# Output projections between the layers of a two-block network: seven half-size fp32 products instead of eight, the token tiles in two pairs

## The reference

```python
for layer in range(4):          # mixers: latent attention, window attention, Hyena, latent attention
    hx = rmsnorm(x, g_pre[layer]) * (1.0 + scale_x) + shift_x       # same for ctx
    yx, yc = mixer(hx, hc, ..., w_out)     # ends in (o * silu(gate)) @ w_out, w_out is 1024 x 1024
    x = x + gate_x * rmsnorm(yx, g_post[layer])
    ctx = ctx + gate_c * rmsnorm(yc, g_post[layer])                 # not in the last layer
```

## Time and profile before

| what | value |
|---|---|
| median of 3 runs | 1885.49 us (1885.35 to 1885.64) |
| span of the profiled execution | 1879.6 us, so 5.9 us below the median of the runs |
| TensorE busy | 1825.9 us, 97% |
| VectorE busy | 824.3 us, 44% |
| ScalarE busy | 412.2 us, 22% |
| GpSimd busy | 65.8 us, 4% |
| matmuls of L714 | 166.6 us |
| DMA queue | 366.36 MB |

### The profile page before, as it was taken

How to read it: one execution, slowest core, us unless ns; L and a number is a source line. 1 busy time by engine, 2 the same in 40 slices (tenths; PEclk the granted TensorE clock), 3 DMA queues, 4 the chain that set the end, 5 groups by cost and what they waited for, 6 DMA issues and landing times.

```text
span 1879.6 us, 18030 instructions
## 1 busy us (share of the span) xinstructions
PE 1825.9 (97%) x6829; PEld 960.0 (51%) x6829; DVE 824.3 (44%) x2070; ACT 412.2 (22%) x1011; POOL 65.8 (4%) x82
## 2 busy tenths in 40 slices
PE   6999999999999999999899999999999999999997
PEld 2545564444454744443345855588854443443432
DVE  4874545773775666527953233363441010010001
ACT  2121342102772222112212223222111111111111
POOL 0000000000100000004500000000010000000000
PEclk9999999999999999999999999999999999999999
DMA  9754100552100534321203330534487999999993
GB/s 403 263 208 181 45 1 23 213 204 109 68 1 14 208 113 157 123 101 45 73 1 146 133 124 1 201 124 151 157 352 293 427 428 427 428 427 428 428 427 166
DMA packets 31398, 367.57 MB, mean 196 GB/s; under 512 B 3675, under 2 KB 3788, under 8 KB 6348
## 3 DMA queue, kind: packets, MB, share of 16 engines
q1 hardware_dynamic: 31308, 366.36, 48.7%
HBM read 365.26 MB, written 1.09 MB: 195 GB/s over the span
## 4 chain that ended last, share of the span: by engine, by line
PE 93%; DVE 4%; ACT 1%; issue 1%; DMA 1%; POOL 0%; SPq 0%; DVEq 0%; ACTq 0%; POOLq 0%
PE bank L812 14%; PE bank L2967 12%; PE bank L714 9%; PE bank L1790 8%; PE bank L3004 6%; PE bank L1620 4%; PE bank L1337 3%; PE bank L2988 3%; PE bank L895 3%; PE bank L2942 3%; PE bank L2265 2%; PE bank L1465 2%; PE bank L917 2%; PE bank L1175 1%; PE bank L2771 1%; PE bank L1503 1%
## 5 line engine op out<-in xcount | busy, mean ns | idle before, releaser
L812 PE MATMUL bank<-hT,slot 128*128 128x256 f32 (+1 forms) x832 | 268.1, 478 | 0.4 <-DVE open_o L835 0.4
L812 PEld LDWEIGHTS bank<-hT,slot 128*128 128x128 f32 x832 | 156.0, 190 | 97.7 <-issue 85.0
L407 DVE SCALAR_TENSOR_TENSOR product<-slot,cond_rows 128x1024 f32<-128x1024 f32 x160 | 195.6, 1223 | 8.6 <-DVE product L407 3.0
L1790 PE MATMUL bank<-hT,slot 128*128 128x512 f32 (+1 forms) x448 | 168.9, 531 | 0.0
L714 PE MATMUL bank<-slot,gT 128*128 128x512 f32 x384 | 166.6, 592 | 0.0
L3044 DVE SCALAR_TENSOR_TENSOR hT<-hT,bank 128x512 f32<-128x512 f32 x16 | 11.0, 688 | 259.8 <-ACT hT L3079 259.8
L1790 PEld LDWEIGHTS bank<-hT,slot 128*128 128x128 f32 x448 | 83.2, 190 | 70.1 <-issue 67.0
L714 PEld LDWEIGHTS bank<-slot,gT 128*128 128x128 f32 x384 | 72.3, 190 | 88.0 <-issue 87.9
L3004 PE MATMUL bank<-slot,hT 128*64 128x512 f32 x256 | 92.1, 595 | 0.0
L2967 PE MATMUL bank<-slot,scratch 128*64 128x512 f32 x256 | 90.6, 592 | 0.0
L1620 PE MATMUL bank<-slot,hT 128*128 128x512 f32 x192 | 82.7, 592 | 0.0
(11 more groups left out here) (423 smaller groups left out, 2662.3 us busy)
## 6 DMA issues: line engine op xcount, KB each, us to landing
slot<-panels_dram SPq DMA_DIRECT2D x91, 2048.0 KB, 9.7
late_slots<-panels_dram SPq DMA_DIRECT2D x40, 2048.0 KB, 20.4
slot<-panels_dram SPq DMA_DIRECT2D x40, 1024.0 KB, 5.2
branch_slot<-panels_dram SPq DMA_DIRECT2D x9, 2048.0 KB, 23.3
mod_slot<-panels_dram SPq DMA_DIRECT2D x4, 2048.0 KB, 16.4
slot<-panels_dram SPq DMA_DIRECT2D x4, 1536.0 KB, 7.1
gate_rows_all<-gate_rows_dram SPq DMA_DIRECT2D x4, 1024.0 KB, 8.7
slot<-panels_dram SPq DMA_DIRECT2D x2, 1280.0 KB, 18.6
```

What stands on the lines that cost most here:

```text
L407: last = m.nc.vector.scalar_tensor_tensor(out=m.product[:], in0=m.slot(panel)[:, c * D:(c + 1) * D], scalar=1.0, in1=m.cond_rows[:, s, :], ...
L812: last = self.m.nc.tensor.matmul(self.bank(g), self.m.slot(panel)[:, k * width + j * P:k * width + (j + 1) * P], self.m.hT[:, k, 0:self.n] ...
L1790: last = nc.tensor.matmul(bank(g)[:, tokens], m.slot(i)[:, k * 512 + g % 4 * P:k * 512 + (g % 4 + 1) * P], m.hT[:, k, tokens], start=k == ...
```

## The change

The 4 x (512 x 1024) product of tokens and weights is cut into 2x2 blocks: tiles 0 and 2 against tiles 1 and 3, lower against upper half of the 1024 inputs, and left against right half of the 1024 outputs. Seven block products in Winograd's form of Strassen's scheme stand for the eight of before. They need sums and differences of the blocks of both operands and of the products:

- `TokenSums`: VectorE makes four sums of 128x1024 from `m.gT` once all four tiles are there, each waiting for the one before.
- `WeightSums`: GpSimd makes eight sums of 128x1024 from the two weight panels: in `attention` of layer 0, in `window_attention` (one after the sink terms of every second unit, from unit 6 on), and at the end of `conv_rounds`. In the first two they are kept in `COLUMN_SLOT`, so the first two panels of the next layer's `w_mod` are loaded only in `enter_layer`.
- `enter_layer` works on the pair of tiles 0 and 1 (w = 0) and then on tiles 2 and 3 (w = 1). A block product is four matmuls of 128x512. The first product is copied to SBUF by ScalarE (`copy_first`) before TensorE goes on in the same bank (`closing_first`). VectorE adds the products, GpSimd multiplies three of the four result blocks with the gate, ScalarE squares and makes `normed`. The roots are taken for a pair at once.
- Tiles 2 and 3 are both left over: `turn_last` turns both, at `g == 4` instead of `g == 2` in `window_inputs` and `latent_inputs`, and still before the fourth half group in `conv_inputs`. All turns use banks 6 and 7 now, so each waits until the one before has been taken.

The core of the diff:

```diff
+class TokenSums:
+    def __init__(self, m, tokens, spare):
+        self.m, self.tokens = m, tokens
+        self.ready = m.sig("token_sums_ready")
+        self.second, self.third, self.fourth = spare
+        self.at = self.ready.total
+    def block(self, high, odd):
+        return self.tokens[:, 4 * high:4 * high + 4, :].rearrange("p k (s t n) -> p t k s n", s=2, t=2)[:, odd]
+    def make(self, dve):
+        v, ready = self.m.nc.vector, self.ready
+        v.tensor_tensor(self.third, self.block(0, 0), self.block(0, 1), ALU.subtract).then_inc(ready.sem, ready.one())
+        dve.wait_ge(ready.sem, self.at + 1)
+        v.tensor_tensor(self.block(0, 1), self.block(0, 1), self.block(1, 1), ALU.add).then_inc(ready.sem, ready.one())
+        dve.wait_ge(ready.sem, self.at + 2)
+        v.tensor_tensor(self.second, self.block(0, 1), self.block(0, 0), ALU.subtract).then_inc(ready.sem, ready.one())
+        dve.wait_ge(ready.sem, self.at + 3)
+        v.tensor_tensor(self.fourth, self.block(1, 0), self.second, ALU.subtract).then_inc(ready.sem, ready.one())
+    def wait(self, eng, n):
+        eng.wait_ge(self.ready.sem, self.at + n)
...
+    def make(self, pool, piece):
+        kind, part = divmod(piece, 2)
+        g = self.m.nc.gpsimd
+        if kind == 0:
+            last = g.tensor_tensor(self.first[part], self.block(1, 0, part), self.block(0, 0, part), ALU.subtract)
+        elif kind == 1:
+            pool.wait_ge(self.ready.sem, self.at + part + 1)
+            last = g.tensor_tensor(self.second[part], self.block(1, 1, part), self.first[part], ALU.subtract)
+        elif kind == 2:
+            pool.wait_ge(self.ready.sem, self.at + part + 1)
+            last = g.tensor_tensor(self.block(1, 0, part), self.block(1, 1, part), self.block(1, 0, part), ALU.subtract)
+        else:
+            pool.wait_ge(self.ready.sem, self.at + 2 + part + 1)
+            last = g.tensor_tensor(self.fourth[part], self.block(0, 1, part), self.second[part], ALU.subtract)
+        last.then_inc(self.ready.sem, 1)
...
+            if t >= 1:
+                pe.wait_ge(by_dve.sem, turned_by_dve + t)
+                pe.wait_ge(by_act.sem, turned_by_act + t)
...
+            def closing_first(w):
+                m.tile_of_gT(pe, 2 * w)
+                pe.wait_ge(opened.sem, opened.at(w + 1))
+                for k in range(4):
+                    last = nc.tensor.matmul(low[w][:, :], tile(4 + k, 2 * w), upper(0, k), start=False, stop=k == 3,
+                                            skip_group_check=True)
+                last.then_inc(ready.sem, ready.one())
...
+            def of_second(w):
+                tokens.wait(pe, 3)
+                weights.wait(pe, 2)
...
+            opening(0)
+            m.last_tile(pe)
+            closing_first(0)
+            of_second(0)
+            gate_rows.turn(pe)
+            of_first(0)
+            of_third(0)
+            of_fourth_tokens(0)
+            of_fourth_weights(0)
+            m.tile_of_gT(pe, 2)
+            opening(1)
+            closing_first(1)
+            of_second(1)
+            of_first(1)
+            pe.wait_ge(gate_rows.copied.sem, gate_rows.copied.at(1))
+            turn(pe, 0)
+            of_third(1)
+            turn(pe, 1)
+            of_fourth_tokens(1)
+            of_fourth_weights(1)
+            def turn_last(pe):
+                turn(pe, 2)
+                turn(pe, 3)
+            m.late_turn = turn_last
...
+            sum_sixth(0)
+            sum_fifth(0)
+            sum_last_block(0)
+            sum_second_block(0)
+            sum_third_block(0)
+            root_products(0)
+            add_residual(0)
+            gate_first(1)
+            root_rows(0)
+            sum_sixth(1)
+            sum_fifth(1)
+            take_turned(0)
+            sum_last_block(1)
+            take_turned(1)
+            sum_second_block(1)
+            sum_third_block(1)
+            root_products(1)
+            add_residual(1)
+            root_rows(1)
+            take_turned(2)
+            take_turned(3)
...
+            copy_first(0)
+            square_first_block(0)
+            gate_rows.copy(act)
+            square_blocks(0)
+            square_third_block(0)
+            copy_first(1)
+            square_rows(0)
+            square_first_block(1)
+            square_rows(1)
+            normalise(0)
+            take_turned(0)
+            take_turned(1)
+            square_blocks(1)
+            square_third_block(1)
+            square_rows(2)
+            square_rows(3)
+            normalise(1)
+            take_turned(2)
+            take_turned(3)
...
+            m.earlier(pool, gate_rows.landed)
+            for w in range(2):
+                pool.wait_ge(squares.sem, squares.at(4 * w + 2))
+                nc.gpsimd.tensor_tensor(fifth[w], fifth[w], gate(w, 1), ALU.mult).then_inc(gated.sem, gated.one())
+                pool.wait_ge(squares.sem, squares.at(4 * w + 3))
+                nc.gpsimd.tensor_tensor(sixth[w], sixth[w], gate(w, 1), ALU.mult).then_inc(gated.sem, gated.one())
+                pool.wait_ge(squares.sem, squares.at(4 * w + 4))
+                nc.gpsimd.tensor_tensor(first[w], first[w], gate(w, 0), ALU.mult).then_inc(gated.sem, gated.one())
...
+                columns.all_taken(pool, len(columns.work))
+                weights.loaded(pool)
+                for piece in range(weights.PIECES):
+                    weights.make(pool, piece)
...
+                if step >= FIRST_SUM and step % 2 == 0 and (step - FIRST_SUM) // 2 < weights.PIECES:
+                    weights.make(pool, (step - FIRST_SUM) // 2)
...
-                if g == 2:
+                if g == 4:
...
-        groups = [(n, t) for n in range(3) for t in range(NT)]
+        groups = [(n, t) for pair in range(2) for n in range(2) for t in (2 * pair, 2 * pair + 1)] + [(2, t) for t in range(NT)]
```

More of the change, by code:

```diff
@@ new lines, in of_second, with of_first @@
+            def of_second(w):
+                tokens.wait(pe, 3)
+                weights.wait(pe, 2)
+                for k in range(4):
+                    last = nc.tensor.matmul(middle[w][:, :], tokens.second[:, k, w, :], weights.column(weights.second, k),
+                                            start=k == 0, stop=k == 3)
+                last.then_inc(ready.sem, ready.one())
+            def of_first(w):
+                for k in range(4):
+                    last = nc.tensor.matmul(high[w][:, :], tile(k, 2 * w + 1), weights.column(weights.first, k),
+                                            start=k == 0, stop=k == 3)
+                last.then_inc(ready.sem, ready.one())
@@ new lines, in of_third, with of_fourth_tokens @@
+            def of_third(w):
+                weights.wait(pe, 3)
+                pe.wait_ge(summed.sem, summed.at(5 * w + 1))
+                for k in range(4):
+                    last = nc.tensor.matmul(middle[w][:, :], tokens.third[:, k, w, :], lower(1, k), start=False, stop=k == 3,
+                                            skip_group_check=True)
+                last.then_inc(ready.sem, ready.one())
+            def of_fourth_tokens(w):
+                tokens.wait(pe, 4)
+                pe.wait_ge(summed.sem, summed.at(5 * w + 2))
+                for k in range(4):
+                    last = nc.tensor.matmul(high[w][:, :], tokens.fourth[:, k, w, :], upper(1, k), start=False, stop=k == 3,
+                                            skip_group_check=True)
+                last.then_inc(ready.sem, ready.one())
@@ L699, in _, with of_fourth_weights @@
+            def of_fourth_weights(w):
+                weights.wait(pe, 4)
+                pe.wait_ge(summed.sem, summed.at(5 * w + 3))
+                for k in range(4):
+                    last = nc.tensor.matmul(middle[w][:, :], tile(4 + k, 2 * w + 1), weights.column(weights.fourth, k),
+                                            start=False, stop=k == 3, skip_group_check=True)
+                last.then_inc(ready.sem, ready.one())
             for i in out_panels:
@@ L724, in _ @@
         @block.scalar
         def _(act):
+            junk = m.scratch[:, 0, 0:512]
             def take_turned(t):
```

309 lines of the change are left out of this document (202 added, 107 removed).

## The result

The changed kernel takes **1913.07 us** (median of 4 runs, 1911.04 to 1913.95) where the kernel before takes 1885.42 on the same chip: ratio 1.0148, 95% interval [1.0133, 1.0162], 27.7 us slower. Its profiled execution has a span of 1911.0 us.

What follows compares the result with a forecast made beforehand. The prediction took TensorE's work and waits as the bound (93% of the chain). Its terms, -20.6 + 4.4 + 14.0 + 13.9 + 11 + 5 = +27.7 us, gave 1913 us, with a range of 1889 to 1924.

Steps and rivals of the forecast that it cites:

- Removed products: Projections in three calls: six block products of 3.43 us leave TensorE's path, -20.6 us.
- Openings: First block products: TensorE waits about 0.87 us for ScalarE's copy at five places, 4.4 us.
- Entries: Next layer's entry: TensorE waits 5.45 us in layer 1, 3.7 in layer 2, 4.85 in layer 3; together 14.0.
- Token sums: After the Hyena layer: GpSimd's sums alternate with VectorE's operations, so the second product waits 13.9 us.
- Window attention: GpSimd's eight weight sums shut out VectorE's scaling, costing TensorE 11 us, bounds 0 and 20.
- the scaling is not shut out: Rival on window attention: the one-tensor scaling runs on, attention costs nothing, 1902 us; chance 0.2.
- Layer 0: Layer 0's eight weight sums run well ahead of the attention and meet copies from PSUM: cost nothing.
- Clock: TensorE's granted clock drops behind three of the new waits (layer 1, layer 3, token sums): 5 us, bounds 0 and 7.
- The 5.9 us between span and median: Gap between profiled span and median of the runs, added to the predicted span of 1907.3 to give 1913 us.

Runs made afterwards that it cites:

- all_mended_2: Changed kernel with half_sums, hold_gpsimd and early_turns edits, both first products opened before either closes, VectorE's product sums moved earlier: 1867.32 us, ratio 0.9901.
- early_turns: Changed kernel, but in layers 1 and 3 tiles 2 and 3 are turned ahead of the third and fourth group, not both ahead of the fifth: 1898.16 us.
- slow_scaling: Changed kernel, but the window attention's scaling also keeps its row's largest element as accumulated output, which is no fast form: 1908.18 us.
- half_sums: Changed kernel, but window attention makes sixteen weight sums of 128x512, one behind each unit, instead of eight of 128x1024: 1903.07 us.
- hold_gpsimd: Changed kernel, but after the Hyena layer GpSimd holds its last four weight sums until VectorE has made three token sums: 1902.41 us.
- three_mended: Changed kernel with the edits of half_sums, hold_gpsimd and early_turns together: 1877.14 us, ratio 0.9953.
- first_products_2: Changed kernel with only the new TensorE order (both first products opened before either closes) and VectorE's product sums moved earlier: 1897.44 us.

## Why the prediction was right

The forecast was 1913 and slower; the terms, by the stretches above and the starts in TensorE's timeline:

- **Removed products**, -20.6: right, seen bare in all_mended_2 (56.91 against 56.92).
- **Openings**, 4.4: five gaps of 0.78 to 0.84 us idle, with the drain some 1.0 by the starts, 4.9. The rows that the prediction took its 0.87 from give 0.80 (281.59 + 0.60 - 281.39).
- **Entries**, 5.45, 3.7 and 4.85: the waits are 1.69 + 3.56, 2.27 + 1.69 and 1.69 + 2.80, so 5.25, 3.96 and 4.49. Their mechanism is shown for layers 1 and 3 by early_turns. For layer 2 it rests on the timeline alone: the row was late by 2.27 us; no edit of that chain was tried.
- **Token sums**, 13.9: 983.97 - 968.73 - 3.44 = 11.8 us. The alternation was as told (L345 to L355 at 2.26 to 2.38 us), but four sums came behind the last gating instead of five, since GpSimd had four done by 971.0.
- **Window attention**, 11: 10.0. The reason was the one on record: the rival "the scaling is not shut out" falls by the 2.24 us of two scalings in the timeline above, slow_scaling shows that the fast form is the reason, and half_sums that the sums cost nothing by themselves. That the size fits is luck. The prediction had VectorE lose 20 us, 2.5 for each sum, and some 9 of them covered; VectorE's scaling lost 13.7, 1.7 for each, and 3.7 were covered. Part of the 10.0 shows as slower work: in the stage TensorE is idle for 5.7 us more than before and busy for 4.3 us more, at a granted clock of 0.94 instead of 0.98. No run shows whether that clock lay on the path while VectorE was behind. The prediction's list of what to look for called this scaling L1241; that is the latent attention's line, in the window attention it is L1383. L1241 never met a large sum.
- **Layer 0**, 0: the stretch is 229.07 against 229.06.
- **Clock**, 5 with bounds 0 and 7: too small. What the waits leave of the four stretches is 2.1, 2.1 and 2.1 us at the entries (7.34 - 5.25, 6.04 - 3.96, 6.62 - 4.49, each without the extra turn) and 2.2 behind the Hyena layer, 8.5 in all. About 1.1 of it, by the starts, is the drain at the six gaps of the entries, and 7.4 is work at the lower level: the granted clock is 0.50 to 0.52 in the worst 2 us behind each of the four places. So the price of about 1.7 for each was right (2.2 behind the Hyena layer), and what made the term too small is that layer 2's waits were left out of it.

The terms as measured are -20.6 + 4.9 + 13.7 + 11.8 + 10.0 + 8.5 = +28.3, the medians differ by 27.7, the sum on record was 27.7. The order of the terms and their reasons were right; that the sum meets the measurement to a tenth is luck, since the misses have both signs (the clock 3.5 too small, the token sums 2.1 and the attention 1.0 too large). The 5.9 us between span and median were not what lies around a span, as they were taken to be. Only some 2 us do (the changed kernel's profiled run: 1913.0 against 1911.0). The rest is that the profiled execution of before was among the quickest: spans of its other executions lie between 1878.8 and 1888.2. So the spans of the two profiles differ by 31.4 and not by 27.7, and that the 5.9 led to the right median is luck as well.

## What to carry to other kernels

Saving TensorE's work is worth its full price only where each product's inputs are ready in time: here 20.6 us of matmuls were bought with 49 us of waits and lower clock, and taking most of these away by order and piece size, with every sum still made, gave a kernel 1% faster than the one before (ratio 0.9901). Work given to an idle GpSimd is not free to VectorE: keep each piece shorter than VectorE's work on PSUM that runs beside it, and keep it away from the moment at which VectorE has a chain of small operations. When a product is moved forward on TensorE, look for the sum that frees its next bank on VectorE, and move that too.

## What the runs showed of the hardware

The clock behind a wait does not follow from the length of the wait. Behind the same wait at the same place, hold_gpsimd (3.25 us) and three_mended (3.26 us) had different clocks. Windows of hold_gpsimd, then of three_mended (length; busy PE, PEld, DVE, ACT, POOL; granted clock):

```profile
971.00:973.00 2.00, 0.82 (x2) 0.00 (x0) 1.93 (x4) 0.69 (x2) 0.00 (x0) 1.00 0.00 0
973.00:975.00 2.00, 0.00 (x0) 0.00 (x0) 1.97 (x2) 0.00 (x0) 0.00 (x0) 0.72 0.00 0
975.00:977.00 2.00, 1.93 (x3) 0.90 (x4) 1.84 (x3) 0.00 (x0) 1.91 (x1) 0.50 0.03 8
977.00:979.00 2.00, 2.00 (x4) 0.95 (x3) 0.00 (x0) 0.00 (x0) 2.00 (x2) 0.50 0.00 0
```

```profile
955.00:957.00 2.00, 0.50 (x2) 0.00 (x0) 1.97 (x2) 0.69 (x2) 0.00 (x0) 1.00 0.00 0
957.00:959.00 2.00, 0.24 (x1) 0.25 (x2) 1.93 (x3) 0.00 (x0) 0.22 (x1) 1.00 0.00 0
959.00:961.00 2.00, 2.00 (x5) 0.81 (x5) 1.56 (x2) 0.00 (x0) 2.00 (x1) 1.00 0.00 0
```

In the first the clock fell to 1.2 GHz (0.50) and the eight records behind the wait took 6.49 us, in the second it stayed at 2.4 GHz and they took 3.70. Why is open: in both, TensorE had worked for 14.0 us without a gap up to the wait, behind the same gap of 0.55 us. One kernel's own executions differ in the same way: the five of first_products_2 took 1896.83 to 1897.44 us at a mean granted clock of 0.989 to 0.990, or 1904.86 and 1905.27 at 0.986. A term for the clock should carry 0 and some 3 us as the bounds of each wait of this length. Second, for an operation of VectorE with one source in SBUF the form decides whether GpSimd shuts it out: a scaling of 512 elements with an accumulated output (0.745 us) passes under GpSimd's sums, the plain one (0.483) doesn't. Operations with two sources in SBUF are shut out too (L345 to L355, 2.26 to 2.38 us), those that read PSUM are not (in half_sums L1375 takes its 0.74 us under L718). Third, an operation of 16 elements pays as much for it as a large one: it waits for a whole sum (2.27 us for L346, 0.17 where GpSimd is held back).
